# A norm in front of the last block's first matmuls: four weight tiles taken from unscaled halves, the factor put on their results, and three smaller edits with it

## The reference

```python
out = merge_branches(z, (y_a, y_b, y_c), w_branch[l], w_out[l])   # ... @ w_out
x_new = x + gt[:, None] * rms_norm(out, norm_post[l])
...
def rms_norm_2(x, g):
    y = xf * lax.rsqrt(jnp.mean(xf * xf, axis=-1, keepdims=True) + NORM_EPS)
    return (y * g.astype(jnp.float32)).astype(x.dtype)
```

## Time and profile before

| | us |
|---|---|
| median of 3 runs | 1456.33 (1455.81 to 1456.39) |
| the profiled execution: its own time | 1457.11 |
| its span in the profile | 1455.8 |
| PE busy | 1390.5 |
| DVE, ACT, POOL busy | 922.0, 684.7, 32.7 |
| mean granted clock of PE | 0.989 |

### The profile page before, as it was taken

How to read it: one execution, slowest core, us unless ns; L and a number is a source line. 1 busy time by engine, 2 the same in 40 slices (tenths; PEclk the granted TensorE clock), 3 DMA queues, 4 the chain that set the end, 5 groups by cost and what they waited for, 6 DMA issues and landing times.

```text
span 1455.8 us, 21302 instructions
## 1 busy us (share of the span) xinstructions
PE 1390.5 (96%) x8556; PEld 1182.1 (81%) x8556; DVE 922.0 (63%) x1625; ACT 684.7 (47%) x1182; POOL 32.7 (2%) x42
## 2 busy tenths in 40 slices
PE   5999999999999999989999999998999999999998
PEld 2676668777888888659879899996988998888998
DVE  5545764676533344488776778557667767888546
ACT  5433544224322222454455454465656756666434
POOL 0000000000000000100000000010000002000000
PEclk9999999999999999999999999999999999999999
DMA  9331443144323222522234355553643345555552
GB/s 368 133 101 49 151 149 115 44 145 162 107 88 112 90 87 87 191 105 88 73 116 145 102 197 191 190 184 97 200 148 109 102 145 167 198 188 194 194 175 73
DMA packets 57795, 202.37 MB, mean 139 GB/s; under 512 B 6272, under 2 KB 9536, under 8 KB 57696
## 3 DMA queue, kind: packets, MB, share of 16 engines
q1 hardware_dynamic: 55568, 194.01, 39.3%
q0 software_dynamic: 1760, 6.25, 1.3%
q10 hardware_dynamic: 368, 0.74, 0.1%
HBM read 199.93 MB, written 1.05 MB: 138 GB/s over the span
## 4 chain that ended last, share of the span: by engine, by line
PE 86%; DVE 8%; ACT 3%; DMA 1%; issue 1%; ACTq 0%; SPq 0%; DVEq 0%
PE gemm_bank L415 17%; PE gemm_bank L417 17%; PE gemm_bank L416 17%; PE misc_bank L415 5%; PE misc_bank L416 5%; PE misc_bank L417 5%; PE misc_bank L426 3%; PE gemm_bank L426 3%; PE misc_bank L427 1%; PE gemm_bank L427 1%; DVE wlo L1716 1%; PE misc_bank L862 1%; PE misc_bank L821 1%; PE gemm_bank L504 1%; PE misc_bank L847 1%
## 5 line engine op out<-in xcount | busy, mean ns | idle before, releaser
L1716 DVE TENSOR_TENSOR wlo<-raw,whi 128x1024 fp32r<-128x1024 f32 x316 | 383.2, 1224 | 77.5 <-ACT whi L1206 73.7
L1206 ACT ACTIVATE whi<-raw 128x1024 fp32r<-128x1024 f32 x316 | 332.7, 1055 | 174.0 <-PE gemm_bank L417 104.2
L415 PE MATMUL gemm_bank<-halves,wlo 128*128 128x256 f32 (+1 forms) x1152 | 374.6, 325 | 22.1 <-DVE halves L2178 5.9
L417 PE MATMUL gemm_bank<-halves,whi 128*128 128x256 f32 (+1 forms) x1152 | 359.0, 312 | 0.0
L416 PE MATMUL gemm_bank<-halves,whi 128*128 128x256 f32 (+1 forms) x1152 | 359.0, 312 | 0.0
L415 PEld LDWEIGHTS gemm_bank<-halves,wlo 128*128 128x128 f32 x1152 | 221.4, 192 | 48.0 <-issue 22.4
L417 PEld LDWEIGHTS gemm_bank<-halves,whi 128*128 128x128 f32 x1152 | 221.7, 192 | 12.1
L416 PEld LDWEIGHTS gemm_bank<-halves,whi 128*128 128x128 f32 x1152 | 221.9, 193 | 11.2 <-issue 0.7
L415 PE MATMUL gemm_bank<-arena_r,wlo 128*128 128x256 f32 (+1 forms) x408 | 133.2, 326 | 1.5 <-issue 1.0
L417 PE MATMUL gemm_bank<-arena_r,whi 128*128 128x256 f32 (+1 forms) x408 | 132.5, 325 | 0.0
L416 PE MATMUL gemm_bank<-arena_r,whi 128*128 128x256 f32 (+1 forms) x408 | 132.5, 325 | 0.0
(11 more groups left out here) (408 smaller groups left out, 2215.7 us busy)
## 6 DMA issues: line engine op xcount, KB each, us to landing
raw<-in_stream SPq DMA_DIRECT2D x348, 512.0 KB, 3.4
arena<-in_stream SPq DMA_DIRECT2D x16, 512.0 KB, 11.8
x<-in_x SPq DMA_DIRECT2D x1, 1024.0 KB, 6.4
x<-in_ctx SPq DMA_DIRECT2D x1, 1024.0 KB, 9.9
y<-in_hy_decay POOLq DMA_DIRECT2D x2, 512.0 KB, 4.6
arena<-in_gm_ws POOLq DMA_DIRECT2D x2, 512.0 KB, 6.6
const_b<-in_const_b POOLq DMA_DIRECT2D x1, 763.0 KB, 6.8
y<-in_hy_w POOLq DMA_DIRECT2D x2, 256.0 KB, 4.1
```

The costliest lines, as they stand in the source:

```text
L415: mm(out, w_lo, r_hi, start=first, stop=False)
L417: return mm(out, w_hi, r_hi, start=False, stop=last)
L1206: act.activation(self.whi[:, t % SPLIT, :], self.raw_tile(t), ACT.Copy).then_inc(*self.mark("tile_hi", "tile_hi", t))
L1716: dve.tensor_tensor(self.wlo[:, t % SPLIT, :], self.raw_tile(t), self.whi[:, t % SPLIT, :].bitcast(F32), ALU.subtract).then_inc(*self.mark ...
```

## The change

1. `wout` in both layers: ACT writes the square before the branch_out copies.
2. Between the two layers one weight tile's `dve_lo` moves from between two reciprocals into the loop that makes the halves, at k = 3.
3. The norm of x at the start of the second block is no longer waited for. In the loop that makes x, ACT writes a hi half of x·g_mix (`raw_hi`) and DVE its lo half (`dve_raw_half`), without the norm's factor. PE (`pe_late_norm`) takes zc0, zc1, head 0 and head 1 together in the order QUAD, which interleaves tiles and rows so that work can begin with row 0, and puts the eight sums of squares between the steps LATE_SUMS. Two weight tiles' `dve_lo` stand in and ahead of that loop.
4. The factor, one number per token, is held in `mix_r`. DVE multiplies it onto the results of zc0, zc1 and heads 0 to 5 as they leave PSUM; for the heads ACT then reads that product (`late_head`) where it read PSUM.
5. The scaled halves, which heads 6 and on use, are made one row at a time behind the eight cmp tiles.
6. DVE does both compressor inputs ahead of the evacuation of the heads that stand behind them; `pe_head(0)` follows the four joined tiles and so stands ahead of head 2.
7. `down` uses side-by-side halves too. The low half of each bank is copied out by ACT (`act_down_low`), DVE adds it to the bank and multiplies in an instruction of its own, and POOL adds the result to x.

```diff
+LATE_HEADS = 6
+LATE_SUMS = (1, 3, 6, 10, 17, 19, 21, 23)
...
+        self.mix_r = self.sq_sum[:, TOK:ALL]
...
-                m = self.three(self.out_banks[o][:, 0:TOK], hi[:, c], lo[:, c], self.ah[:, j, :], self.al[:, j, :], j == 0, j == FT - 1)
+                pe.matmul(self.out_banks[o][:, :], hi[:, c], self.ah_al[:, j, :], start=(j == 0), stop=False)
+                m = pe.matmul(self.out_banks[o][:, 0:TOK], lo[:, c], self.ah[:, j, :], start=False, stop=(j == FT - 1))
...
+    def pe_late_norm(self):
+
+        quad, n = self.tiles[self.pe_next:self.pe_next + 4], 0
+        for step, (i, k) in enumerate(QUAD):
+            T = quad[i]
...
+            if k == n:
+                self.pe.wait_ge(*self.at("raw_half", k))
+                n += 1
...
+            m = self.three(self.G[T.use % 4][:, 0:TOK], self.whi[:, s, w], self.wlo[:, s, w], self.hi(k, 1), self.lo(k, 1), k == 0, k == KT - 1)
...
+            if step in LATE_SUMS:
+                self.pe_sum(("res", 1), LATE_SUMS.index(step), TOK)
...
-        self.pe_tiles(2)
-        self.pe_heads(3)
+        self.pe_head(0)
+        self.pe_heads(1)
...
+            self.act_sq(("out", l), j, n, b[:, 0:n]).then_inc(*self.mark("act_sq", "sq", ("out", l), j))
             for s in range(n // TOK):
                 t = slice(s * TOK, (s + 1) * TOK)
...
-            self.act_sq(("out", l), j, n, b[:, 0:n]).then_inc(*self.mark("act_evac", "evac", T.use))
...
+        elif kind == "head" and j < LATE_HEADS:
+            act.wait_ge(*self.at("evac", T.use))
...
+        if kind == "cmp":
+            self.act_hn("g_mix", self.cmp_row(T))
...
+        self.act_hi()
         for k in range(KT):
             act.wait_ge(*self.at("x_new", l, k))
+            act.activation(self.hi(k, 1), self.x[:, k, 0:n], ACT.Copy, scale=self.c["g_mix"][:, k:k + 1]).then_inc(*self.mark("act_half", "raw_hi", k))
...
+        elif kind == "zc":
+            dve.wait_ge(*self.at("used", T.t))
+            dve.tensor_tensor(self.Z[:, 4 + j, :], b[:, 0:TOK], self.mix_r, ALU.mult).then_inc(*self.mark("dve_evac", "evac", T.use))
         elif kind == "head":
+            if j < LATE_HEADS:
+                dve.wait_ge(*self.at("used", T.t))
...
+                dve.tensor_tensor(self.late_head(j), b[:, 0:TOK], self.mix_r, ALU.mult).then_inc(*self.mark("dve_evac", "evac", T.use))
...
+            if s == 0 and k == 3:
+                self.dve_lo()
...
         self.dve_cross_rstd(("out", 0), 1)
-        self.dve_lo()
         self.dve_cross_rstd(("res", 0), 0)
...
+        self.dve_lo()
         self.dve_rstd(("out", l), n)
         for k in range(KT):
+            if k == 4:
+                self.dve_lo()
...
+            if k:
+                self.dve_raw_half(k - 1)
+        self.dve_raw_half(KT - 1)
...
-        self.dve_hn("g_mix")
-        self.dve_tiles(2)
+        v.wait_ge(*self.at("root", ("res", 1)))
+        v.reciprocal(self.mix_r, self.mix_r).then_inc(*self.mark("dve_rstd", "rstd", ("res", 1)))
+        v.wait_ge(*self.at("rstd", ("res", 1)))
+        self.dve_tiles(2, split=False)
         self.dve_compress("k")
...
+                v.tensor_tensor(t, self.out_banks[o][:, 0:TOK], self.tmp[:, 3 + i % 2, TOK:ALL], ALU.add).then_inc(*self.mark("dve_out", "down_r", o))
                 v.wait_ge(*self.at("down_r", o))
-                v.tensor_tensor(self.x[:, o, 0:TOK], self.x[:, o, 0:TOK], self.tmp[:, 3 + (i - 1) % 2, 0:TOK], ALU.add).then_inc(*self.mark("dve_x", "dacc", o))
+                v.tensor_tensor(t, t, self.tmp[:, 2, 0:TOK], ALU.mult).then_inc(*self.mark("dve_scaled", "down_scaled", o))
...
+            pool.tensor_tensor(self.x[:, o, 0:TOK], self.x[:, o, 0:TOK], self.tmp[:, 3 + i % 2, 0:TOK], ALU.add).then_inc(*self.mark("pool_x", "dacc", o))
```

More of the change, by code:

```diff
@@ L465, in pe_feature @@
         elif T.l:
-            h_hi, h_lo = ([half(k, 0) for k in range(KT)] for half in (self.hi, self.lo))
+            side = 1 if T.kind == "head" and T.j < LATE_HEADS else 0
+            h_hi, h_lo = ([half(k, side) for k in range(KT)] for half in (self.hi, self.lo))
         else:
@@ L509, in pe_tile @@
         elif kind in ("k", "q", "hy", "gu", "gate", "esel", "zc", "head", "wout", "wout2", "pgate"):
-            begun = {"k": ("h", T.l), "wout": ("merged", T.l), "zc": ("hn", "g_mix"), "wout2": ("merged", 2), "pgate": ("hn", "g_ple")}.get(kind)
+            begun = {"k": ("h", T.l), "wout": ("merged", T.l), "wout2": ("merged", 2), "pgate": ("hn", "g_ple")}.get(kind)
             if kind == "pgate" and j == 3:
                 pe.wait_ge(*self.at("rstd", "g_ple"))
+            if kind == "head" and j == LATE_HEADS:
+                begun, lead = ("hn", "g_mix"), True
             m = self.pe_feature(T, self.pe_bank(T.use), hi, lo, begun if lead else None)
@@ L1234, in act_tile @@
                     self.also("rows", l, g)
-        elif kind in ("k", "q", "zc"):
+        elif kind in ("k", "q"):
             act.wait_ge(*self.at("used", T.t))
-            dst = {"k": self.K, "q": self.Q}[kind][:, j, 0:n] if kind != "zc" else self.Z[:, 4 + j, :]
-            act.activation(dst, b[:, 0:n], ACT.Copy).then_inc(*self.mark("act_evac", "evac", T.use))
+            act.activation({"k": self.K, "q": self.Q}[kind][:, j, 0:n], b[:, 0:n], ACT.Copy).then_inc(*self.mark("act_evac", "evac", T.use))
         elif kind in ("v", "gv", "vm", "vsg"):
@@ L1294, in act_tile @@
             self.also("head_zsq", j)
-        elif kind == "cmp" and j[1] == 3:
+        if kind == "cmp":
+            self.act_hn("g_mix", self.cmp_row(T))
+        if kind == "cmp" and j[1] == 3:
             act.wait_ge(*self.at("used", T.t))
@@ L1494, in act_h_sum, with late_head, hn_slot, cmp_row @@
         m.then_inc(*self.mark("act_h", "h_sum", 0, k))
-    def act_hn(self, gain):
-        for k in range(KT):
-            self.act.wait_ge(*self.at("hn_sum", gain, k))
-            self.act.activation(self.hi(k, 0), self.tmp[:, (0, 1, 3, 4)[k % 4], 0:TOK], ACT.Copy).then_inc(*self.mark("act_half", "hn_hi", gain, k))
+    def late_head(self, j):
+        return self.tmp[:, 4, (j % 2) * TOK:(j % 2 + 1) * TOK]
+    def hn_slot(self):
+        return self.tmp[:, 2, TOK:ALL]
+    def cmp_row(self, T):
+        return 4 * ("k", "v").index(T.j[0]) + T.j[1]
+    def act_hn(self, gain, k):
+        self.act.wait_ge(*self.at("hn_sum", gain, k))
+        self.act.activation(self.hi(k, 0), self.hn_slot(), ACT.Copy).then_inc(*self.mark("act_half", "hn_hi", gain, k))
     def act_cross_sq(self, s, k):
@@ L1674, in act_block2 @@
         self.act_tiles(FT)
+        act.wait_ge(*self.at("used", self.act_done - 1))
+        for i in range(2):
+            self.act_down_low(i)
         for i, o in enumerate(self.DORDER):
+            if i + 2 < KT:
+                self.act_down_low(i + 2)
             act.wait_ge(*self.at("dacc", o))
@@ L2564, in gpsimd_program @@
         self.pool_sums("g_ffn", TOK)
+        for i, o in enumerate(self.DORDER):
+            pool.wait_ge(*self.at("down_scaled", o))
+            pool.tensor_tensor(self.x[:, o, 0:TOK], self.x[:, o, 0:TOK], self.tmp[:, 3 + i % 2, 0:TOK], ALU.add).then_inc(*self.mark("pool_x", "dacc", o))
     def sync_program(self):
```

66 lines of the change are left out of this document (42 added, 24 removed).

## The result

The changed kernel took 1467.07 us (median of 4 runs, 1466.04 to 1467.64) against 1456.36 for the kernel before (4 runs): a ratio of 1.0066, 95% interval 1.0053 to 1.008, which is 9.6 us (7.7 to 11.7). The forecast was 1466.3, from the median of before. The profiled execution took 1466.04 us with a span of 1464.6, 8.9 and 8.8 above those of before.

What follows compares the result with a forecast made beforehand. PE, busy 1390.5 of 1455.8 us, was taken as the bound, so new PE waits cost in full. Between layers -1.1, norm +11.8, down -2.4, tail +1.7 gave +10.0: 1466.3 us, range 1460 less 1 to 1470.5.

Steps and rivals of the forecast that it cites:

- Four joined tiles, second wait: Late norm: joined tiles end eight us earlier, at r 21.5; then PE waits 6.6 us for pe_head(0), leaving 1.4.
- cmp tiles and pe_head(3): Cmp k tiles paced by DVE at 2.43, PE losing 1.8; pe_head(3) then waits 4.3 to 4.8 instead of 1.42, +3.0.
- the balance of +5.6: Norm's loss without clock: +0.4 at head 3's start, +3.4 after pe_head(3)'s wait, +5.6 with cmp v and head 6.
- Clock: Half clock behind the norm's three longer waits (4.4, 6.6, 4.5 us): charged 2.7, 2.6 and 0.9, together +6.2.
- the sentence that before had paid 2.8 us for it in zc0: Kernel before: zc0's 24 matmuls take 5.3 us, not 2.9, so half clock cost about 2.8, already within the 29.5.
- The sign that the prediction used for a harmless wait: Waits of 1.42 and 2.07 us were followed by full speed, so none of length 2 us drops the clock.
- Between the layers: Turn between layers: two ACT copies leaving the chain's front give -0.9, the moved wlo 0.2 more, together -1.1.
- 0.2 on the path: Between the layers: the moved wlo, standing between two reciprocals while ACT's root was coming, cost only 0.2 us.
- The bound of -2.1: Between the layers: the larger gain, if the moved wlo's whole 1.15 counts.
- down: Down's 176 joined groups of two take 0.346 against 0.36 for three: -2.4, bounds 0 and -2.7.
- Behind down: Tail: DVE waits for POOL's additions, a row about 1.42, first pgate matmul +1.7 later; +0.8 if side by side.
- The sum: Whole kernel: -1.1 + 11.8 (norm) - 2.4 + 1.7 = +10.0 on the profiled execution, 1466.3 on the median.

Runs made afterwards that it cites:

- b1_head_first: Changed kernel, with head 0 evacuated and head 2's wlo made ahead of the keys' compressor input on DVE, head 0 ahead of four copies on ACT; ratio 1.0046 to before.
- d2_late_fill: Late norm reordered on PE and DVE, scaled halves spread out, idle matmuls ahead of joined and cmp k tiles, parts 1, 2 and 7 kept; ratio 0.9995 to before.
- b3_no_scaled: Changed kernel without DVE's scaled halves behind the cmp tiles, ACT writing an unscaled copy of x instead (wrong results); ratio 1.0061 to before, 4 runs.
- b2_fill: Changed kernel with idle matmuls (10, 14 and 9) inside PE's three waits of the late norm; ratio 1.0025 to the kernel before.
- d0_fill_before: Kernel before with idle matmuls (11, 8 and 8) between the layers and in the last norm's two waits, part of the computation changed; ratio 1.0013 to before.
- a1_down: Kernel before with part 7 alone (joined down, low half copied by ACT, x summed by POOL); ratio 0.9997 to before.
- e1_best: Parts 1, 2 and 7 on the kernel before, plus nine idle matmuls in the wait between the layers; ratio 0.9986 to before.

## Why the forecast held, step by step

- **Four joined tiles, second wait.** Shown. First product at 5.9 behind the sum (5.6 foretold from nearly the same zero), four tiles done at 24.7 (24 foretold at the low clock) and at 21.7 without the clock's part (21.5), pe_head(0) without the clock's part at 28.5 (28.1). b1_head_first and d2_late_fill show that the order on DVE and ACT makes the wait.
- **cmp tiles and pe_head(3).** The mechanism is shown: 0.69 and 0.89 us lost on the last two tiles (0.8 and 1.0 foretold), and b3_no_scaled takes the pace away. The size depends on what is taken as before. b2_fill and d0_fill_before, both with a full clock, differ by 124.8 - 119.2 = 5.6 us at the wait near 1100, just the balance of +5.6, but d0_fill_before lost 1.1 us there to a late weight tile. Against a1_down it is 124.8 - 118.0, about 6.7. The equality with 5.6 is luck in part.
- **Clock.** The sum of +6.2 was 6.9 (2.7, 2.6 and 0.9 foretold; 2.8, 2.6 and 1.5 measured by b2_fill). But the sentence that before had paid 2.8 us for it in zc0 was wrong. It took a PE that is busy at a low clock for a PE that sets the pace; "DVE makes the halves faster than that" was not worked out, and eight rows of DVE's are as long as zc0 took. The error did no harm, since the sum started from the measured 29.5. The sign that the prediction used for a harmless wait was no sign either: the 2.07 us wait behind down, followed by full speed in before, is followed by half clock in three other profiles of that code.
- **Between the layers.** -1.1 was mis-sized: -1.8 in the profile after. The step that failed is "0.2 on the path" for the moved wlo. DVE's first reciprocal ended, and ACT's root had landed, as that wlo began (648.19); moving it let the second reciprocal start 1.0 sooner, and PE's wait fell from 5.17 to 4.15. The bound of -2.1 was nearer. That the slow PE covers the wlo at its new place was right: from the wait on, 84.95 us before and 85.00 after, both with 6.8 us of half clock.
- **down.** -2.4 was right for the profiled execution. Six of the ten profiles with joined matmuls show -1.2.
- **Behind down.** +1.7 against 0.5 + 0.9 = 1.4 in this profile, 2.0 in a1_down, of which 0.8 is the clock that before's profile was spared. The row was 1.27, not 1.42: only some of the two engines' instructions lengthen each other.
- **The sum.** +10.0 was foretold on the profile, +8.9 came, but before's profile held 1.4 us of half clock ahead of 1100 that is not the norm's. On the median it was +10.7, by the ratio +9.6. The norm's part alone was 12.3 in these two profiles and 13.7 against a before without that stretch, where 11.8 was foretold: stalls 6.7 for 5.6, clock 6.9 for 6.2. So the path, the waits and the clock drops were right. That the total came within 1 us is partly luck, since the norm was put 1.9 too low and the gain between the layers 0.7 too low, which offset each other in part.

## What to carry to other kernels

Work that is taken ahead of a factor gains nothing by itself if the next instruction on the waiting engine needs the factor: first follow who fetches the early results, and what stands ahead of that fetch in its engine's order. Here the joined tiles were done eight us sooner (at the full clock), and seven of them were gone at the next wait. What brought them back was filled waits (6.0 us in b2_fill) and another order on DVE and ACT, and even so the late norm gained nothing.

Count the low clock behind a wait as a term of its own, but only where PE then sets the pace: a busy share of 1.00 at half clock does not say that it does. And do not read from one profile whether a wait drops the clock, or what a stretch costs: look for a half clock in the kernel before as well as in the one after.

## What the runs showed that was not expected

- The joined matmuls have two paces at the full clock, in the same code: 0.3467 us a group in four profiles (down 61.0), 0.353 in six (62.1), each for the whole of down, while the same groups of the feed-forward layer ahead of it took 0.3467 in all ten. Three matmuls of 256 columns took 0.360 in all. No run tells why.
- Idle matmuls kept the granted clock at its full level through all waits that they filled, and the filled wait between the layers was worth 2.5 us in place, though its end came no sooner by it.
- Twelve runs of one kernel on one chip lie up to 11 us apart (1451.0 to 1462.37 for e1_best). In the profiles much of such differences lies in places that no edit touched: 157.0 or 159.9 us in the stretch that holds the wait near 270, 251.75 or 253.2 in the one ahead of down, and 0, 1.4 or 3.0 us ahead of the wait near 1100. Each of the longer ones has a stretch at half clock there. What sets it off is not shown.
